# Feed-forward's second product: two of eight row pairs by seven block products in place of eight

## The chip, the cores and the metric

The kernel runs on one core of a Trainium2 chip. The metric is the device time of one execution in microseconds. Engines are named as in the profile: PE is the matrix engine (TensorE), PEld its weight loads, DVE is VectorE, ACT is ScalarE, SP is SyncE, whose queue issues the DMA transfers of the weights.

## The reference

One layer of an encoder over 256 tokens with a width of 2048. Only its last part matters here:

```python
def squared_relu_mlp(h, w1, w2):
    return jnp.square(jax.nn.relu(h @ w1)) @ w2
...
        x = x + squared_relu_mlp(rms_norm(x, norm_ffn_g[l]), w_ff1[l], w_ff2[l])
    return rms_norm(x, final_norm_g)
```

`w_ff1` is 2048 x 8192 and `w_ff2` is 8192 x 2048, both float32. Ahead of it come a gated convolution branch, an attention branch and a cross-attention, which the change leaves alone.

## The kernel before

Float32 products are made of three products in the format fp32r. Each operand is split into a high part (a rounded copy) and a low part (what is left); a product is high x high + high x low + low x high, all summed in PSUM.

**Units and the ring.** All weights pass through a ring of four slots (`RING = 4`) as units of 512 KB: two rows of 128 of the weight matrix, 512 columns wide, hence 1024 elements in each of 128 partitions. For each unit, in order:

1. SP loads it into `raw` (`load`, L372). Slot `u % 4` of `raw` is free when the low part of unit u - 4 is made (semaphore `lo_ready`).
2. ACT makes the high part `whi` (`hi`, L561). It waits for the load and for PE to be done with unit u - 4 (semaphore `used`).
3. DVE makes the low part `wlo` (`lo`, L931).
4. PE multiplies (`unit`, L1418 to L1420): 2 rows x 2 token halves x 3 products, 12 matmuls of 512 columns.

Every engine has one program order, written out by hand. ACT and DVE are three units ahead of PE (`LEAD = 3`): at step k of a stretch they split unit k + 3.

**Feed-forward.** The 8192 hidden columns are taken in four groups of 2048 (`GROUPS`). In each group the first product (`still_unit`, L1827 and L1829) takes 4 chunks of 8 units. Between it and the second product stand a few wide operations for each chunk: ACT's `ff_take` (L859), DVE's `ff_add` (L1324) and `ff_relus` (L1331), ACT's `ff_squares` and `ff_high`, DVE's `ff_low_part` (L1336). They leave the split hidden values in `c_hi` and `c_lo`, 16 tiles of 128 hidden columns x 256 tokens. The second product takes 4 chunks of 512 output columns, each 8 units, each chunk in two PSUM banks of its own, one for each half of the tokens. After each chunk DVE adds its two banks to the residual `xres` (L1375). In the last group the very last chunk is ordered so that the first token half ends earlier (`last_chunk`), and the final normalization follows it.

Of the kernel before, what the change touches and what calls it, by code (L numbers as in the profile page):

```python
# [7 lines left out]
ALU = mybir.AluOpType  # L8
# [120 lines left out]


def pair_of(n):

    return (n + 1) % 2
# [38 lines left out]
def build(nc, x, mem, positions, norm_mix_g, w_in, b_gate, conv_w, conv_b, conv_ln_g, conv_ln_b,  # L172
# [9 lines left out]
    with ExitStack() as ctx:  # L182
# [36 lines left out]
        fin_g = at(o + 8192, "fin_g", [P, D])  # L219
        fin = at(o + KS, "fin", [P, TT, D])  # L220

        o = cursor[0]
# [24 lines left out]
        rs_row = at(o, "rs_row", [P, SEQ])  # L247
        rs_diag = at(o + 1024, "rs_diag", [P, TT, P])

        o = cursor[0]  # L250
# [42 lines left out]
        def sem(name):  # L293
            return ctx.enter_context(nc.semaphore(name))
# [44 lines left out]
        rs_spread, rs_turned, rs_row_ready = (sem(n) for n in ("rs_spread", "rs_turned", "rs_row_ready"))  # L339
        ff_low, ff_sum, ff_relu, ff_square, ff_hi, ff_lo = (sem(n) for n in ("ff_low", "ff_sum", "ff_relu", "ff_square", "ff_hi", "ff_lo"))  # L340
        fin_landed, fin_gained = sem("fin_landed"), sem("fin_gained")
        tail_used, tail_added, tail_squared, tail_summed = (sem(n) for n in ("tail_used", "tail_added", "tail_squared", "tail_summed"))
# [25 lines left out]
        def _(sp):  # L368
            def load(u, r, src, kts=2, width=NC):

                wait(sp, lo_ready, u - RING + 1 + r)
                sp.dma_start(raw[:, u % RING, 0:kts * width].rearrange("p (k n) -> p k n", k=kts),  # L372
                             src).then_inc(landed[u % RING], 16)
# [55 lines left out]
            for n, (c, u) in enumerate(XO_ORDER):  # L429
                load(U_XO + n, 0, w_xo[:, 2 * u:2 * u + 2, NC * c:NC * (c + 1)])  # L430
            with sp.Fori(0, GROUPS) as g:
                r = g * FF_UNITS
                for c in range(CH):
                    load_chunk(U_FF + UPC * c, r, w_ff1, g * D + NC * c)
                for c in range(CH):
                    for k in range(UPC):
                        load(U_FF + UPC * (CH + c) + k, r, w_ff2[:, ds(g * KT + 2 * k, 2), NC * c:NC * (c + 1)])

# [116 lines left out]
        def _(act):  # L555
            def hi(u, r=0):

                s = u % RING
                act.wait_ge(landed[s], 16 * (u // RING + 1) + r * (16 // RING))
                wait(act, used, u - RING + 1 + r)  # L560
                act.activation(whi[:, s, :], raw[:, s, :], ACT.Copy).then_inc(hi_ready, 1)  # L561

            def turn_out(turn, dst, k0, gain=None, banks=(0, 1), first=6):
# [303 lines left out]
            def ff_high(c, done):  # L867
                act.wait_ge(ff_square, done)
                act.activation(c_hi[:, CPB * c:CPB * (c + 1), :], ff_row[:, c % 2, :, :], ACT.Copy).then_inc(ff_hi, 1)

            def ff_group(g, r, last, first=False):
                for c in range(CH):
                    for k in range(UPC):
                        hi(U_FF + UPC * c + k + LEAD, r)
                        if first and c == 0 and k == 1:
                            turn_out(T_X2 + CH - 1, a_hi, 4 * (CH - 1), V_FFN)
                        if first and c == 0 and k == 2:
                            x2_squares(CH - 1)
                        if first and c == 0 and k == 4:
                            act.wait_ge(sum_ready, 3)  # L880
                            root(sd_n, ss_sum, D)
                        if first and c == 0 and k == 7:
                            act.wait_ge(rs_turned, 1)
                            act.activation(rs_row[:], ps[:, 4, 0:SEQ], ACT.Copy, scale=float(D)).then_inc(rs_row_ready, 1)
                        if c and k == 1:
                            ff_squares(c - 1, g * CH + c)
                        if c and k == 2:
                            ff_high(c - 1, g * CH + c)
                    act.wait_ge(used, r + (U_FF + UPC * (c + 1)))
                    if c >= 2:  # L890
                        act.wait_ge(ff_lo, g * CH + (c - 1))
                    ff_take(c)
                for c in range(CH):
                    for k in range(UPC):
                        if not last or UPC * (CH + c) + k + LEAD < FF_UNITS:
                            hi(U_FF + UPC * (CH + c) + k + LEAD, r)
                        if c == 0 and k == 1:
                            ff_squares(CH - 1, g * CH + CH)
                        if c == 0 and k == 2:
                            ff_high(CH - 1, g * CH + CH)  # L900
                    if last and c < CH - 1:
                        act.wait_ge(chunk_out, N_FF + g * CH + c + 1)
                        chunk_squares(sq_res, xres[:, :, NC * c:NC * (c + 1)], c, SS_2 + TT * c)

# [21 lines left out]
        def _(dve):  # L926
            def lo(u, r=0):

                s = u % RING
                dve.wait_ge(hi_ready, u + 1 + r)  # L930
                dve.tensor_tensor(wlo[:, s, :], raw[:, s, :], whi[:, s, :].bitcast(F32), ALU.subtract).then_inc(lo_ready, 1)  # L931

            def bank_blocks(b):
# [399 lines left out]
            def ff_low_part(c, done):  # L1333
                dve.wait_ge(ff_hi, done)
                k = slice(CPB * c, CPB * (c + 1))
                dve.tensor_tensor(c_lo[:, k, :], ff_row[:, c % 2, :, :], c_hi[:, k, :].bitcast(F32), ALU.subtract).then_inc(ff_lo, 1)  # L1336

            def ff_group(g, r, last, first=False):
                for c in range(CH):
                    for k in range(UPC):  # L1340
                        if c and k == 0:
                            ff_add(c - 1, g * CH + c)
                        lo(U_FF + UPC * c + k + LEAD, r)
                        if first and c == 0 and k == 1:
# [12 lines left out]
                        if c and k == 2:  # L1357
                            ff_low_part(c - 1, g * CH + c)
                for c in range(CH):
                    for k in range(UPC):  # L1360
                        if c == 0 and k == 0:
                            ff_add(CH - 1, g * CH + CH)
                        if not last or UPC * (CH + c) + k + LEAD < FF_UNITS:
                            lo(U_FF + UPC * (CH + c) + k + LEAD, r)
                        if c == 0 and k == 0:
                            ff_relus(CH - 1, g * CH + CH)
                        if c == 0 and k == 2:
                            ff_low_part(CH - 1, g * CH + CH)
                        if last and k == 4 and c:

                            gain(c - 1)
                    if not last or c < CH - 1:
                        dve.wait_ge(used, r + (U_FF + UPC * (CH + c + 1)))
                        cols = xres[:, :, NC * c:NC * (c + 1)]
                        dve.tensor_tensor(cols, ps[:, 2 * c:2 * c + 2, :], cols, ALU.add).then_inc(chunk_out, 1)  # L1375

# [31 lines left out]
        def _(pe):  # L1408
# [392 lines left out]

            def last_chunk():
                p = 2 * (CH - 1)
                for k in range(UPC // 2):
                    unit(U_END - UPC + k, 0, c_hi, c_lo, 2 * k, p, k == 0, False)
                for t in range(TT):
                    tok = slice(P * t, P * (t + 1))
                    for k in range(UPC, KT):
# [5 lines left out]
                        mm = pe.matmul(ps[:, p + t, :], c_lo[:, k, tok], w_hi, start=False, stop=(k == KT - 1))  # L1814
                    mm.then_inc(tail_used, 1)

            def still_unit(u, r, k0, first, last, c):
# [14 lines left out]
            def ff_group(g, r, first=False, last=False):  # L1832
                for c in range(CH):
                    if c == 0:
                        pe.wait_ge(chunk_out, N_XO + 3 if first else g * CH + (N_FF - CH + 2))
                    elif c == 1:
                        pe.wait_ge(chunk_out, N_XO + CH if first else g * CH + N_FF)
                        if first:
                            pe.wait_ge(rs_row_ready, 1)
                    else:  # L1840
                        pe.wait_ge(ff_sum, g * CH + (c - 1))
                    for k in range(UPC):
# [6 lines left out]
                        if first and c == 0 and k == 6:  # L1849
# [3 lines left out]
                            mm.then_inc(rs_turned, 1)  # L1853
                for c in range(CH - last):
                    if c != 1:
                        pe.wait_ge(ff_sum, g * CH + (CH - 1 if c == 0 else CH))
                    for k in range(UPC):
                        if c == 0 and k % 2 == 0:
                            pe.wait_ge(ff_lo, g * CH + (k // 2 + 1))
                        unit(U_FF + UPC * (CH + c) + k, r, c_hi, c_lo, 2 * k, 2 * c, k == 0, k == UPC - 1)  # L1860

# [3 lines left out]
            ff_group(GROUPS - 1, (GROUPS - 1) * FF_UNITS, last=True)  # L1865
            last_chunk()

# [27 lines left out]
```

## Time and profile before

| | |
|---|---|
| median of 3 runs | 1624.31 us (1624.09 to 1624.81) |
| the profiled execution | 1623.88 us, its span 1622.1 us |
| PE busy | 1612.4 us (99% of the span) |
| DVE busy | 1102.8 us (68%) |
| ACT busy | 817.7 us (50%) |
| DMA | 304.97 MB, mean 188 GB/s |
| granted PE clock over the span | 0.999 |

The span is what the profile shows, from the first instruction to the last; the execution's own time is 1.8 us longer. Busy shares say how much of the span an engine had work. Which engine sets the time is read from the waits: an engine with no waits of its own is the bound.

### The profile page before, as it was taken

The page shows a single profiled execution, that of the slowest core. Times are in us where ns is not written, and L with a number is a line of the kernel's source. Part 1 is how long each engine was busy: PE and PEld are TensorE (multiplying, and loading weights), DVE is VectorE, ACT ScalarE, POOL GpSimd, SP SyncE. Part 2 cuts the span into 40 slices and gives each one's busy share as a digit, 9 for nine tenths or more (in the row PEclk, how much of TensorE's full clock was granted, in tenths as well). Part 3 has the DMA queues.
Part 4 walks back from the last instruction along what each step waited for, and adds up shares of the span by engine and source line. Part 5 has one row for each costly group of instructions (what it writes and reads, how often), then busy time and mean ns, then how long its engine had stood idle before and what let it go on. Part 6 is the DMA issues. An engine that isn't in the chain of part 4 may idle for free.

```text
span 1622.1 us, 22880 instructions
## 1 busy us (share of the span) xinstructions
PE 1612.4 (99%) x8210; PEld 1373.9 (85%) x8210; DVE 1102.8 (68%) x1494; ACT 817.7 (50%) x1046; POOL 70.6 (4%) x156
## 2 busy tenths in 40 slices
PE   9999999999999999999999999999999999999998
PEld 7888888888888888888889888888888888888886
DVE  5688889888888898665556656555555555546655
ACT  6444456555555556744446655334443454335543
POOL 6500010000000000000000000000000000000000
PEclk9999999999999999999999999999999999999999
DMA  7666655555555666667664566666666666666664
GB/s 250 203 190 186 189 160 170 174 176 179 177 163 175 216 201 192 185 191 254 188 193 146 167 185 193 194 195 182 195 194 192 187 188 194 193 191 192 185 189 145
DMA packets 161292, 304.97 MB, mean 188 GB/s; under 512 B 11689, under 2 KB 20513, under 8 KB 160801
## 3 DMA queue, kind: packets, MB, share of 16 engines
q1 hardware_dynamic: 160128, 300.45, 61.1%
q0 software_dynamic: 1056, 3.46, 0.6%
q8 instruction: 52, 0.85, 0.2%
q14 instruction: 24, 0.20, 0.0%
q10 hardware_dynamic: 32, 0.01, 0.0%
HBM read 301.78 MB, written 2.10 MB: 187 GB/s over the span
## 4 chain that ended last, share of the span: by engine, by line
PE 99%; ACT 0%; DVE 0%; DMA 0%; issue 0%; ACTq 0%
PE ps L1418 21%; PE ps L1420 21%; PE ps L1419 21%; PE ps L1827 15%; PE ps L1829 7%; PE ps L1431 1%; PE ps L1577 1%; PE ps L1576 1%; PE ps L1575 1%; PE ps L1630 1%; PE ps L1629 1%; PE ps L1600 0%; PE ps L1599 0%; PE ps L1598 0%; PE ps L1593 0%; PE ps L1592 0%
## 5 line engine op out<-in xcount | busy, mean ns | idle before, releaser
L931 DVE TENSOR_TENSOR wlo<-raw,whi 128x1024 fp32r<-128x1024 f32 x560 | 684.1, 1224 | 413.1 <-ACT whi L561 411.9
L561 ACT ACTIVATE whi<-raw 128x1024 fp32r<-128x1024 f32 x560 | 591.4, 1060 | 590.2 <-PE ps L1420 417.9
L1827 PE MATMUL ps<-a_both,whi 128*128 128x512 f32 x1024 | 321.7, 395 | 0.0
L1418 PE MATMUL ps<-whi,c_hi 128*128 128x512 f32 x752 | 293.3, 390 | 0.0
L1420 PE MATMUL ps<-whi,c_lo 128*128 128x512 f32 x752 | 292.6, 389 | 0.0
L1419 PE MATMUL ps<-wlo,c_hi 128*128 128x512 f32 x752 | 292.6, 389 | 0.0
L1418 PE MATMUL ps<-whi,a_both 128*128 128x512 f32 x700 | 277.1, 396 | 0.0
L1419 PE MATMUL ps<-wlo,a_both 128*128 128x512 f32 x700 | 272.7, 390 | 0.0
L1420 PE MATMUL ps<-whi,a_both 128*128 128x512 f32 x700 | 272.7, 390 | 0.0
L1829 PEld LDWEIGHTS ps<-a_both,wlo 128*128 128x128 f32 x1024 | 192.4, 188 | 45.4
L986 DVE SCALAR_TENSOR_TENSOR acc<-hconv,cwk,acc 128x256 f32<-128x256 f32 x464 | 205.0, 496 | 13.2 <-PE ps L1630 13.2
L1829 PE MATMUL ps<-a_both,wlo 128*128 128x256 f32 x1024 | 201.2, 278 | 0.0
L1420 PEld LDWEIGHTS ps<-whi,c_lo 128*128 128x128 f32 x752 | 141.2, 188 | 29.5
L1419 PEld LDWEIGHTS ps<-wlo,c_hi 128*128 128x128 f32 x752 | 141.2, 188 | 29.0
L1418 PEld LDWEIGHTS ps<-whi,c_hi 128*128 128x128 f32 x752 | 141.2, 188 | 28.5
L1827 PEld LDWEIGHTS ps<-a_both,whi 128*128 128x128 f32 x1024 | 156.2, 189 | 0.3
L1420 PEld LDWEIGHTS ps<-whi,a_both 128*128 128x128 f32 x700 | 131.4, 188 | 27.7
L1419 PEld LDWEIGHTS ps<-wlo,a_both 128*128 128x128 f32 x700 | 131.6, 188 | 25.8
L1418 PEld LDWEIGHTS ps<-whi,a_both 128*128 128x128 f32 x700 | 131.6, 188 | 25.8
L1324 DVE TENSOR_TENSOR ff_row<-ps,ff_row 128x1024 f32<-128x1024 f32 x16 | 19.6, 1225 | 24.4 <-ACT ff_row L859 24.4
L859 ACT ACTIVATE ff_row<-ps 128x1024 f32<-128x1024 f32 x16 | 16.4, 1026 | 27.3 <-PE ps L1829 27.3
L722 ACT ACTIVATE probs<-probs,stat 128x128 f32<-128x128 f32 (+1 forms) x32 | 17.2, 538 | 25.1 <-DVE stat L1104 25.1
(275 smaller groups left out, 1342.6 us busy)
## 6 DMA issues: line engine op xcount, KB each, us to landing
raw<-in_w_ff_dram SPq DMA_DIRECT2D x256, 512.0 KB, 4.0
raw<-in_w_in_dram SPq DMA_DIRECT2D x144, 512.0 KB, 3.7
raw<-in_w_mla_out_dram SPq DMA_DIRECT2D x32, 512.0 KB, 4.4
raw<-in_w_conv_out_dram SPq DMA_DIRECT2D x32, 512.0 KB, 4.3
raw<-in_w_out_dram SPq DMA_DIRECT2D x32, 512.0 KB, 4.3
raw<-in_w_ukv_dram SPq DMA_DIRECT2D x16, 512.0 KB, 3.8
raw<-in_w_xkv_dram SPq DMA_DIRECT2D x16, 512.0 KB, 3.9
raw<-in_w_uq_dram SPq DMA_DIRECT2D x16, 384.0 KB, 3.5
```

What stands on the lines that cost most here:

```text
L561: act.activation(whi[:, s, :], raw[:, s, :], ACT.Copy).then_inc(hi_ready, 1)
L722: act.activation(probs[:, h, a:b], probs[:, h, a:b], ACT.Exp, bias=ntop[:, n:n + 1], scale=qs[:, n % TT:n % TT + 1], accum_out=den[:, n:n ...
L859: act.activation(ff_row[:, c % 2, :, :], ps[:, ff1_banks(c), SEQ:], ACT.Copy).then_inc(ff_low, 1)
L931: dve.tensor_tensor(wlo[:, s, :], raw[:, s, :], whi[:, s, :].bitcast(F32), ALU.subtract).then_inc(lo_ready, 1)
L986: ins = dve.scalar_tensor_tensor(out=to, in0=h[:, tap:tap + SEQ], scalar=cwk[:, tap:tap + 1], in1=to, op0=ALU.mult, op1=ALU.add)
L1324: dve.tensor_tensor(row, ps[:, ff1_banks(c), 0:SEQ], row, ALU.add).then_inc(ff_sum, 1)
L1418: pe.matmul(sum_, x_hi[:, k0 + k, tok], w_hi, start=(first and k == 0), stop=False)
L1419: pe.matmul(sum_, x_hi[:, k0 + k, tok], w_lo, start=False, stop=False)
L1420: mm = pe.matmul(sum_, x_lo[:, k0 + k, tok], w_hi, start=False, stop=(last and k == kts - 1))
L1431: tr = pe.transpose(ps[:, first + b, SEQ * (k % 2) + P * t:SEQ * (k % 2) + P * (t + 1)], src[:, t, c0 + P * k:c0 + P * (k + 1)], ident[:])
L1827: pe.matmul(both, whi[:, s, cols[n]], a_both[:, :, k0 + k, :], start=(first and k == 0), stop=False)
L1829: mm = pe.matmul(ps[:, b0 + b + n, 0:SEQ], wlo[:, s, cols[n]], a_hi[:, k0 + k, :], start=False, stop=(last and k == 1))
```

## The change

The 16 units of two neighbouring chunks (a "pair", p = 0 or 1 in each group) are taken together, in an order of their own, `FF2_ORDER`; an entry (c, k) is chunk c of the pair and row k and k + 1 of the group's 16. For rows 0 to 3 (two row pairs, m = 0 and 1) the two token halves, the two rows of a pair and the two chunks make 2 x 2 blocks, and their product is made by seven block products in place of eight (Strassen's scheme in the form with 15 additions). The other twelve units are multiplied as before. The second pair of the last group (`plain`) keeps eight products. So seven pairs of eight are changed.

In each changed pair, positions 4 and 8 of the order (`LEFT`) hold the left chunk's units of rows 0, 1 and 2, 3, and positions 5 and 9 (`RIGHT`) the right chunk's. At a LEFT unit PE makes two block products (6 matmuls), at a RIGHT unit one (3 matmuls), and only the second half of a RIGHT unit is split. The other products need sums of weights, made by DVE from the raw units (`w_sums`, then the parts by ACT's `ws_high` and DVE's `ws_low`), and sums of hidden tiles (`h_sums`, made once for a group during the first product). They follow unit 11 (12 matmuls), unit 12 (6) and unit 13 (6). One partial sum goes into both chunks; ACT copies it out of its bank at two moments (`y_out`), and PE waits for these copies before it adds more. DVE adds to the residual in five steps in place of two. Loads 8, 9, 12 and 13 wait longer, since `w_sums` reads the raw slots.

```diff
+FF2_ORDER = ((0, 4), (0, 6), (1, 4), (1, 6), (0, 0), (1, 0), (0, 8), (0, 10),
+             (0, 2), (1, 2), (0, 12), (0, 14), (1, 8), (1, 10), (1, 12), (1, 14))
+LEFT, RIGHT = (4, 8), (5, 9)
+ONES_BANK, LAST_BANK = 4, 5
+FF2_BANKS = ((2, 0), (2, 6))
...
+                for p in range(2):
+                    for i, (c, k) in enumerate(FF2_ORDER):
+                        n = 2 * p + c
+                        after = {8: 6, 9: 6, 12: 11, 13: 11}.get(i, i - RING)
+                        load(U_FF + UPC * CH + FF2_UNITS * p + i, r, w_ff2[:, ds(g * KT + k, 2), NC * n:NC * (n + 1)], later=after - (i - RING))
...
+            def ws_high(g, p, m):
+                act.wait_ge(ws_made, g * 12 + (6 * p + 3 * (m + 1)))
+                for half in (1, 0):
+                    act.activation(ws_hi[m][half][:], w_sum[:, 2 * NC * half:2 * NC * (half + 1)], ACT.Copy).then_inc(ws_hi_ready, 1)
+            def y_out(g, p, n):
+                if n == 0 and p:
+                    act.wait_ge(mixed, g * 6 + 1)
+                act.wait_ge(y_step, g * 6 + (3 * p + n + 1))
+                act.activation(y_copy[:, n, :], ps[:, ONES_BANK, :], ACT.Copy).then_inc(y_copied, 1)
...
+                    for k in range(FF2_UNITS):
+                        n = UPC * CH + FF2_UNITS * p + k + LEAD
+                        if k + LEAD in RIGHT and not plain:
+                            hi_second(U_FF + n, r)
+                        elif not last or n < FF_UNITS:
+                            hi(U_FF + n, r)
...
+                        if k in (3, 8) and not plain:
+                            ws_high(g, p, k // 8)
+                        if k in (9, 12) and not plain:
+                            y_out(g, p, (9, 12).index(k))
...
+            def w_sums(g, p, m, s):
...
+                wait(dve, ws_lo_ready, g * 8 + (4 * p + 2 * m))
+                dve.tensor_tensor(t1_t3.rearrange("p (b n) -> p b n", b=2), right.rearrange("p (b n) -> p b n", b=2), raw[:, s:s + 2, 0:NC],
+                                  ALU.subtract).then_inc(ws_made, 1)
+                dve.wait_ge(ws_made, g * 12 + (done + 1))
+                dve.tensor_tensor(t2, right[:, NC:], t1, ALU.subtract).then_inc(ws_made, 1)
+                dve.wait_ge(ws_made, g * 12 + (done + 2))
+                dve.tensor_tensor(t4, left[:, NC:], t2, ALU.subtract).then_inc(ws_made, 1)
...
+                        if i in RIGHT and not plain:
+                            lo_second(U_FF + u + i, r)
+                        elif not last or u + i < FF_UNITS:
+                            lo(U_FF + u + i, r)
...
+                            if k in (2, 7):
+                                w_sums(g, p, k // 7, (U_FF + u + LEFT[k // 7]) % RING)
+                            if k in (3, 4):
+                                ws_low(g, p, 0, 4 - k)
+                            if k in (8, 9):
+                                ws_low(g, p, 1, 9 - k)
+                            if k == 12:
+                                add_copies(g, p)
+                            if k == 13:
+                                add_ones(g, p)
+                                dve.wait_ge(p4_done, g * 2 + (p + 1))
+                                dve.wait_ge(mixed, g * 6 + (3 * p + 1))
+                                add_chunk(p, 0)
+                            if k == 14:
+                                add_last(g, p)
...
+                    if i == 11:
+                        pe.wait_ge(ws_lo_ready, g * 8 + (4 * p + 3))
+                        pe.wait_ge(y_copied, g * 4 + (2 * p + 1))
+                        for m in range(2):
+                            mm = product(ONES_BANK, *combined(1, m), *weight_sum(2, m), last=(m == 1))
+                        mm.then_inc(y_step, 1)
+                        for m in range(2):
+                            mm = product(banks[0] + 1, *hidden(2 * m + 1, 1), *weight_sum(3, m), last=(m == 1))
+                        mm.then_inc(p4_done, 1)
+                    if i == 12:
+                        pe.wait_ge(ws_lo_ready, g * 8 + (4 * p + 4))
+                        pe.wait_ge(y_copied, g * 4 + (2 * p + 2))
+                        for m in range(2):
+                            mm = product(ONES_BANK, *combined(0, m), *weight_sum(0, m), last=(m == 1))
+                        mm.then_inc(y_step, 1)
+                    if i == 13:
+                        for m in range(2):
+                            mm = product(LAST_BANK, *combined(2, m), *weight_sum(1, m), first=(m == 0), last=(m == 1))
+                        mm.then_inc(p7_done, 1)
```

`product` is three matmuls of 512 columns. In ACT's and DVE's programs, what stands under `if k == ...` comes behind the split of unit k + 3 in the same step.

## Rows read from the trace of the kernel before

**Rows 1.** The page: busy time of the engines, and the chain that ended last.

```profile
PE 1612.4 (99%) x8210; PEld 1373.9 (85%) x8210; DVE 1102.8 (68%) x1494; ACT 817.7 (50%) x1046; POOL 70.6 (4%) x156
...
PE 99%; ACT 0%; DVE 0%; DMA 0%; issue 0%; ACTq 0%
```

**Rows 2.** Who waited for whom, PE alone, whole span, longest first.

```profile
PE ps L1446 <- POOL stat L460: 1.5, 1, 1.5
```

**Rows 3.** Busy time in one chunk of the second product (us, count; clock, DMA).

```profile
1041.26:1063.02 21.76, 21.76 (x98) 18.02 (x97) 10.96 (x9) 8.48 (x9) 0.00 (x0) 1.00 0.64 194
```

**Rows 4.** Timeline around one unit of the second product: start us, us, engine.

```profile
1074.11 1.23 DVE L931 TENSOR_TENSOR wlo<-raw,whi 128x1024 fp32r<-128x1024 f32 x1 [1.50 <-ACT whi L561]
...
1075.47 0.39 PE L1418 MATMUL ps<-whi,c_hi 128*128 128x512 f32 x1
...
1075.49 8.53 SPq L372 DMA_DIRECT2D raw<-in_w_ff_dram  x4
...
1075.73 1.06 ACT L561 ACTIVATE whi<-raw 128x1024 fp32r<-128x1024 f32 x1 [1.66 <-PE ps L1420]
...
1076.83 1.23 DVE L931 TENSOR_TENSOR wlo<-raw,whi 128x1024 fp32r<-128x1024 f32 x1 [1.50 <-ACT whi L561]
...
1078.19 0.39 PE L1418 MATMUL ps<-whi,c_hi 128*128 128x512 f32 x1
```

**Rows 5.** Groups of instructions by line, feed-forward stretch: busy us, mean ns.

```profile
L931 DVE TENSOR_TENSOR wlo<-raw,whi 128x1024 fp32r<-128x1024 f32 x256 | 313.1, 1224 | 279.0 <-ACT whi L561 279.0
L561 ACT ACTIVATE whi<-raw 128x1024 fp32r<-128x1024 f32 x256 | 271.1, 1060 | 325.6 <-PE ps L1420 180.4 <-PE ps L1829 145.1
...
L1336 DVE TENSOR_TENSOR c_lo<-ff_row,c_hi 128x1024 fp32r<-128x1024 f32 x16 | 19.5, 1219 | 0.0
L1375 DVE TENSOR_TENSOR xres<-ps,xres 128x1024 f32<-128x1024 f32 x15 | 18.4, 1225 | 5.6 <-PE ps L1420 5.6
...
L859 ACT ACTIVATE ff_row<-ps 128x1024 f32<-128x1024 f32 x16 | 16.4, 1026 | 27.3 <-PE ps L1829 27.3
L592 ACT ACTIVATE sq_res<-xres 128x512 f32<-128x512 f32 x12 | 7.5, 634 | 8.6 <-DVE xres L1375 8.6
...
L1316 DVE TENSOR_TENSOR fin<-xres,fin_g 128x512 f32<-128x512 f32 x6 | 3.9, 684 | 0.0
```

**Rows 6.** DMA issues on the page, and the summary of the tile `raw`.

```profile
raw<-in_w_ff_dram SPq DMA_DIRECT2D x256, 512.0 KB, 4.0
...
DMA to landing us min/median/max: 3.3/3.9/9.3
```

**Rows 7.** DMA issues near 742 us: KB each, us to landing.

```profile
xres<-in_x_dram SPq DMA_DIRECT2D x1, 2048.0 KB, 9.0
raw<-in_w_conv_out_dram SPq DMA_DIRECT2D x1, 512.0 KB, 4.3
...
raw<-in_w_out_dram SPq DMA_DIRECT2D x1, 512.0 KB, 9.3
```

**Rows 8.** SP's queue in order of time near 742 us.

```profile
742.56 0.47 SPq L423 DMA_DIRECT2D xres<-in_x_dram  x1
743.63 90.73 SPq L372 DMA_DIRECT2D raw<-in_w_out_dram  x32
```

**Rows 9.** Busy time and granted clock (after the engines) at the end.

```profile
1617.00:1618.00 1.00, 0.00 (x0) 0.00 (x0) 0.96 (x4) 0.88 (x2) 0.00 (x0) 0.86 0.00 0
1618.00:1619.00 1.00, 0.00 (x0) 0.00 (x0) 0.13 (x1) 0.45 (x1) 0.00 (x0) 0.50 0.57 197
```

**Rows 10.** Timeline: the last matmul.

```profile
1614.77 0.39 PE L1814 MATMUL ps<-whi,c_lo 128*128 128x512 f32 x1
```

**Rows 11.** Timeline of PE at the start of the program.

```profile
6.36 0.77 PE L1455 MATMUL ps<-whi,a_both 128*128 128x512 f32 x1 [0.70 <-ACT whi L618]
...
7.88 0.78 PE L1455 MATMUL ps<-wlo,a_both 128*128 128x512 f32 x1
...
10.56 0.39 PE L1455 MATMUL ps<-whi,a_both 128*128 128x512 f32 x1
```

More of the change, by code:

```diff
@@ L1358, in ff_group @@
                             ff_low_part(c - 1, g * CH + c)
-                for c in range(CH):
-                    for k in range(UPC):
-                        if c == 0 and k == 0:
-                            ff_add(CH - 1, g * CH + CH)
-                        if not last or UPC * (CH + c) + k + LEAD < FF_UNITS:
-                            lo(U_FF + UPC * (CH + c) + k + LEAD, r)
-                        if c == 0 and k == 0:
+                for p in range(2):
+                    plain = last and p == 1
+                    u = UPC * CH + FF2_UNITS * p
+                    for k in range(FF2_UNITS):
+                        if p == 0 and k == 0:
+                            ff_add(CH - 1, g * CH + CH)
+                        i = k + LEAD
+                        if i in RIGHT and not plain:
+                            lo_second(U_FF + u + i, r)
+                        elif not last or u + i < FF_UNITS:
+                            lo(U_FF + u + i, r)
+                        if p == 0 and k == 0:
@@ L1377, in _ @@
+                    if not plain:
+                        dve.wait_ge(used, r + (U_FF + u + FF2_UNITS))
+                        dve.wait_ge(mixed, g * 6 + (3 * p + 3))
+                        add_chunk(p, 1)
             ff_group(0, 0, False, True)
@@ L1798, in _, with last_pair @@
                     turn(T_X2 + c, xres, NC * c, split_out(T_X2 + c - 1) if c else None)
[L1802 to L1805, printed above, removed]
+            def last_pair():
+                u = U_END - FF2_UNITS
+                for i, (c, k) in enumerate(FF2_ORDER[:FF2_UNITS - 4]):
+                    unit(u + i, 0, c_hi, c_lo, k, FF2_BANKS[1][c], i in (0, 2), i == 11)
+                p = FF2_BANKS[1][1]
                 for t in range(TT):
@@ L1815, in last_chunk, with product, seven_pair, hidden @@
                     mm.then_inc(tail_used, 1)
+            def product(bank, x_hi, x_lo, w_hi, w_lo, first=False, last=False):
+                pe.matmul(ps[:, bank, :], x_hi, w_hi, start=first, stop=False, skip_group_check=True)
+                pe.matmul(ps[:, bank, :], x_hi, w_lo, start=False, stop=False, skip_group_check=True)
+                return pe.matmul(ps[:, bank, :], x_lo, w_hi, start=False, stop=last, skip_group_check=True)
+            def seven_pair(g, r, p):
+                u = U_FF + UPC * CH + FF2_UNITS * p
+                banks = FF2_BANKS[p]
+                def hidden(k, t):
+                    tok = slice(P * t, P * (t + 1))
+                    return c_hi[:, k, tok], c_lo[:, k, tok]
+                def combined(n, m):
+                    return h_hi[:, n, m, :], h_lo[:, n, m, :]
+                def slot(i, half):
+                    cols = slice(NC * half, NC * (half + 1))
+                    return whi[:, (u + i) % RING, cols], wlo[:, (u + i) % RING, cols]
+                def weight_sum(n, m):
+                    cols = slice(NC * (n % 2), NC * (n % 2 + 1))
+                    return ws_hi[m][n // 2][:, cols], ws_lo[m][n // 2][:, cols]
+                for i, (c, k) in enumerate(FF2_ORDER):
+                    pe.wait_ge(lo_ready, u + i + 1 + r)
+                    if p == 0:
+                        pe.wait_ge(ff_lo, g * CH + (k // 4 + 1))
+                    if i in LEFT:
+                        m = LEFT.index(i)
+                        if i == LEFT[0] and p == 0:
+                            pe.wait_ge(ff_sum, g * CH + CH)
+                        if i == LEFT[0] and p:
+                            pe.wait_ge(mixed, g * 6 + 3)
+                        mm = product(ONES_BANK, *hidden(2 * m, 0), *slot(i, 0), first=(m == 0), last=(m == 1))
+                        if m == 1:
+                            mm.then_inc(y_step, 1)
+                        product(banks[0], *hidden(2 * m + 1, 0), *slot(i, 1)).then_inc(used, 1)
+                    elif i in RIGHT:
+                        m = RIGHT.index(i)
+                        pe.wait_ge(h_lo_ready, g + 1)
+                        product(banks[1], *combined(3, m), *slot(i, 1)).then_inc(used, 1)
+                    else:
+                        for n in range(2):
+                            for t in range(TT):
+                                ends = n == 1 and (i == 15 or (i == 11 and t == 0))
+                                mm = product(banks[c] + t, *hidden(k + n, t), *slot(i, n), first=(i in (0, 2) and n == 0), last=ends)
+                        mm.then_inc(used, 1)
+                    if i == 11:
[12 more added lines that the diff above has]
+                            mm = product(ONES_BANK, *combined(0, m), *weight_sum(0, m), last=(m == 1))
+                        mm.then_inc(y_step, 1)
+                    if i == 13:
+                        for m in range(2):
+                            mm = product(LAST_BANK, *combined(2, m), *weight_sum(1, m), first=(m == 0), last=(m == 1))
+                        mm.then_inc(p7_done, 1)
@@ L1853, in ff_group @@
                             mm.then_inc(rs_turned, 1)
[L1854 to L1860, printed above, removed]
+                pe.wait_ge(ff_sum, g * CH + (CH - 1))
+                seven_pair(g, r, 0)
+                pe.wait_ge(chunk_out, g * CH + (N_FF + 1))
+                if last:
+                    last_pair()
+                else:
+                    seven_pair(g, r, 1)
             ff_group(0, 0, True)
```

121 lines of the change are left out of this document (96 added, 25 removed).

## The prediction

> **What bounds the kernel now.** I read the page first: PE is busy in 99% of the span and the chain that ended last lies on PE [rows 1]. Busy time alone does not prove a bound, so next the waits of PE: the longest in the whole span is 1.5 us, before the first weights are there [rows 2]. So a matmul less is time saved, as long as nobody comes late. In one chunk of the second product (21.76 us, 96 matmuls, so 0.2267 us each) DVE works 10.96 us, ACT 8.48, and the transfers take 0.64 of the DMA engines' time [rows 3]. There seems to be room. Whether the room is at the right places the averages don't say; that needs the order of the work.
>
> The timeline shows the rhythm. A unit is 2.72 us of PE (1075.47 to 1078.19). ACT starts on the slot set free 0.26 us after the next unit's first matmul, DVE 0.04 us after ACT's end, SP's next load 0.15 us after DVE's end (1074.11 + 1.23 = 1075.34, load at 1075.49) [rows 4]. So unit u + 4 is split 2.6 us after PE leaves unit u, and PE comes to it 8.2 us after leaving u (three units): cover of 5.6 us. That reserve is what the change spends.
>
> **What it saves.** A changed pair has 12 units of 12 matmuls and 14 block products of 3: 186 for 192. Seven pairs: 42 matmuls x 0.2267 = 9.5 us. The Trainium skill ("TensorE: Matmul & The Clock Gate", Back-to-back issue gap) has 216 ns for 512 columns; by it this would be 9.1 us. The trace decides for 0.2267.
>
> **What it adds to DVE and ACT.** Durations: DVE 1.22 us for 1024 elements, 0.68 for 512; ACT 1.06 and 0.63 [rows 5]. Hence in a changed pair DVE has 14 x 1.22 + 2 x 0.68 of splits, 2 x (1.22 + 2 x 0.68 + 2 x 1.22) of sums and their low parts, 5 x 1.22 of adding out: 34.6 us, and 38.3 in a group's first pair with `ff_add`, `ff_relus` and `ff_low_part`; before, 22 for the pair. PE's pair without waits is 186 x 0.2267 = 42.16 (before 43.52). ACT comes to about 21.6. Neither engine is full, so I cost this work by its place alone. `h_sums` and their split (about 4 x 0.42 + 1.22 on DVE, 1.06 on ACT, an estimate for the 256-element ones) lie in the first product, where nothing is compressed: nothing, covered by that 5.6 us reserve; without cover under 4 us a group.
>
> **Where it waits.** Second pair of a group, time 0 at its first matmul. Without waits PE would come to unit 4 at 10.88, 6 at 12.92, 8 at 18.36, 10 at 20.40, 11 at 23.12: units 4, 5, 8 and 9 are 6, 3, 6 and 3 matmuls long, so six units pass in 9.5 us in place of 16.3, and the reserve is gone by unit 10.
>
> DVE has the half split of unit 5 done at 7.05, then `w_sums` (1.22 + 0.68 + 0.68 and hops of 0.04) to 9.74, low part 6 to 11.01. Load 8 had to wait for that (in the old order it would have waited for low part 4, at 5.3), and 9 and 10 stand behind it. How long a load takes: 3.3 us at least, the feed-forward's median 4.0 [rows 6], 4.3 with more traffic behind it; I take 4.1. Those behind land in order 1.37 us apart: the 2 MB transfer issued at 742.56 landed after 9.0 (751.56), the 512 KB one behind it, issued at 743.63, after 9.3 (752.93) [rows 7, 8]. So 8, 9, 10 land at 15.3, 16.6, 18.0, load 11 (after low part 7, 14.3) at 19.4. Low part 8 is there at 17.6 (needed 18.36), 10 at 20.38 (needed 20.40). Now `w_sums` again stands ahead of low part 11: 20.42 to 23.09, and low part 11 ends at 24.36. PE waits 1.26 us at unit 11.
>
> Then the main step. After unit 11 PE wants `y_copied`. ACT makes that copy at step 9 behind `hi` of unit 12, and load 12 waits for low part 11. The chain is 24.36, load issued 24.51, landed 28.61, high part 29.71, copy 30.38, PE goes on at 30.40. Unit 11 ended at 27.12: a wait of 3.28 us. Behind it stand unit 12's matmuls and everything else on PE. From here 72 matmuls remain, 16.32 us; their operands are early (low part 12 at 30.9, 13 at 33, the second copy at 34.5 for 36). The pair ends at 46.72: 3.20 us more than before.
>
> In a group's first pair `ff_add` and `ff_relus` push low part 6 to 11.52; the same chain then gives low part 11 at 24.87, PE on at 30.91, end at 47.23: +3.71. The `plain` pair also has the late loads 8 and 12, but no short units: low part 12 at about 30.7 for unit 12 at 32.64, so nothing; cover gone only if a load took 2 us more.
>
> Sum: 4 x 3.71 + 3 x 3.20 = +24.4 us (waits of 34 less the 9.5 saved).
>
> **The clock.** PE's array stands still some 3.1 us in each such wait. At the end of the kernel the granted clock fell (0.86 in the slice from 1617, 0.50 after, so from 2.4 to 1.2 GHz at 1617.7) [rows 9], 2.6 us after the last matmul had ended at 1615.16 [rows 10]. A fall here costs matmuls at half speed afterwards. At the start, where matmuls of 512 columns took 0.77 us, they did so from 6.36 until after 7.88 and 0.39 from 10.56 (the clock column doesn't show this) [rows 11]: some 3.7 us of work at the lower level, 1.9 lost. Nothing in between shows how a wait of 3 us inside dense work is treated, so the bounds are none of seven falls (0) and all (13.3 us). I take three, fewer than half, because the wait is only half a us longer than the one fall seen: +5.7. The Trainium skill says in the same page (HAM oscillation) that idle gaps bring the array back to half rate and cost half of the time spent there; by it the direction is the same, and rows 9 agree with the fall.
>
> **Sum.** 24.4 + 5.7 = 30.1 us onto the profiled execution's 1623.88 (its span 1622.1 and 1.8 around it): 1654.0. The median of the runs is 0.43 above that execution, so 1654.4.
>
> **Rivals.**
> 1. Waits as above, clock never or once lower: 1624.3 + 24.4 = 1648.7. For it: waits of 3 us lie between dense stretches. Against: rows 9, 10.
> 2. The clock falls in nearly every wait: 24.4 + 13.3, 1662.
> 3. Shorter fetches: at 3.3 us a load, both waits shrink and the pairs cost 1.6 and 2.1 more: +13.2, 1637.5. Against: three or four loads issued together, not one alone.
> 4. The wait for `y_copied` doesn't bind, since ACT gets to its copy in time. Then the pair loses 3.28 us: -0.08 and +0.43, together +1.5, 1625.8, no change. It would need the time from low part 11 to the copy, 6.0 us in my sum, to be 2.8; the load alone has never taken under 3.3.
> 5. Other side, one mechanism: the ring's reserve lasts, so low part 11 is there before 23.1 and the copy before unit 11 is over. Then only the 42 matmuls count: 1624.3 - 9.5 = 1614.8. It decides where PE goes on after unit 11 before 27.2 (43.52 less 16.32); I have 30.4. For it only the low averages of rows 3.
>
> **Chances.** Forecast case (waits, two to four falls) 0.35; rival 1 0.28; rival 2 0.17; rival 3 0.12; rival 4 0.04; rival 5 0.04. A difference of 0.2% (3.2 us) is about what a measurement of this kernel can tell from none; rival 4 is inside it, rival 5 beyond it on the fast side, all others slower. So faster 0.04, same 0.04, slower 0.92. A load of 4.8 us in place of 4.1 adds 1.4 a pair, 10 in all. The range 1637 to 1664 holds the first four cases but for their edges, at most 0.2 outside. The size hangs on fetch time and clock, the sign on neither.
>
> **What would show it.** In the profile after: PE with two waits in each of seven pairs, about 1.3 us (DVE's low part, unit 11) and 3.3 us (ACT's copy, before the 12 matmuls behind unit 11), nothing in the last pair; pairs 46.7 to 47.2 us long; 42 matmuls fewer; ACT waiting for the load of unit 12; granted clock under 0.999, by 0.5 x 3.7 us for each fall. If PE shows no waits of over 2 us in the changed pairs, the argument is wrong at the order of ACT's copy; if the waits are right and the time isn't, at the clock.

## The result and the profile after

The change makes the kernel slower: 1657.57 us (median of 4 runs, 1654.94 to 1657.80) against 1624.53 us, a ratio of 1.0202 with a 95% interval of 1.0189 to 1.0214. The profiled execution took 1657.75 us, its span 1655.9; before, the span was 1622.1.

The page of the changed kernel, busy time and the chain that ended last, beside [rows 1]:

```profile
PE 1620.6 (98%) x8168; PEld 1373.0 (83%) x8168; DVE 1192.8 (72%) x1605; ACT 849.3 (51%) x1092; POOL 70.8 (4%) x156
...
PE 87%; DMA 4%; DVE 4%; issue 2%; ACT 2%; SPq 0%; ACTq 0%; DVEq 0%
```

PE is still 98% busy, with 42 matmuls fewer (8168 for 8210), and nothing in the busy line says that the kernel lost 33 us. The chain says it: 13% of it now lies off PE.

Who waited for whom, PE alone (us in total, times, longest), beside [rows 2]:

```profile
PE ps L1976 <- ACT y_copy L914: 20.7, 7, 3.2
PE ps L1976 <- DVE wlo L993: 4.9, 7, 0.7
```

Seven waits for the copy and seven for a low part, one of each in every changed pair. The columns give the idle time of an engine whose matmuls overlap; from one matmul's start to the next, the gap before the copy is used is 3.2 to 3.6 us where 0.23 is normal.

The chain in order of time, second pair of the first group (start us, us, what):

```profile
1052.95 1.15 DVE w_sum L1422
...
1055.54 1.15 DVE wlo L993
...
1057.95 6.00 DMA raw<-in_w_ff_dram
1063.98 1.07 ACT whi L586
1065.07 1.23 DVE wlo L993
1066.30 1.15 DVE w_sum L1422
...
1067.47 0.70 DVE w_sum L1425
...
1068.19 0.69 DVE w_sum L1427
1068.89 1.14 DVE wlo L993
...
1070.18 4.20 DMA raw<-in_w_ff_dram
...
1075.37 0.59 ACT y_copy L914
...
1076.09 0.76 PE ps L1976
```

This is the prediction's chain, read from below. PE goes on at 1076.09, after the copy (1075.37), after the high part of unit 12, after its fetch (4.20 us from 1070.18), after low part 11 (1068.89), which stood behind the weight sums (1066.30 to 1068.89), behind low part 10, whose fetch had itself been held by the first sums. From the start of low part 11 to PE's next matmul 7.2 us pass, of which one unit of PE (2.72) is cover. That ACT stood at the fetch, and not PE or DVE at ACT, is this line of ACT's timeline; the copy comes right behind it:

```profile
1074.41 1.06 ACT L586 ACTIVATE whi<-raw 128x1024 fp32r<-128x1024 f32 x1 [3.48 <-DMA raw<-in_w_ff_dram]
```

The timeline of PE at that point:

```profile
1072.47 0.39 PE L1977 MATMUL ps<-wlo,c_hi 128*128 128x512 f32 x1
1072.70 0.39 PE L1978 MATMUL ps<-whi,c_lo 128*128 128x512 f32 x1
1076.09 0.76 PE L1976 MATMUL ps<-ws,h_hi 128*128 128x512 f32 x1 [3.01 <-ACT y_copy L914]
1076.66 0.63 PE L1977 MATMUL ps<-ws,h_hi 128*128 128x512 f32 x1
1077.08 0.63 PE L1978 MATMUL ps<-ws,h_lo 128*128 128x512 f32 x1
```

After the gap from 1072.70 to 1076.09 the matmuls stand 0.42 to 0.43 us apart and no longer 0.23. That is the lower clock. The granted clock (after the busy times of the five engines) in 3 us just behind each of the seven waits:

```profile
1029.50:1032.50 3.00, 3.00 (x13) 2.50 (x14) 3.00 (x4) 2.42 (x3) 0.00 (x0) 1.00 0.84 276
1076.10:1079.10 3.00, 3.00 (x7) 2.42 (x8) 3.00 (x4) 2.58 (x3) 0.00 (x0) 0.50 0.87 278
1215.10:1218.10 3.00, 3.00 (x8) 2.37 (x9) 3.00 (x4) 2.54 (x3) 0.00 (x0) 0.55 0.75 250
1263.40:1266.40 3.00, 3.00 (x7) 2.40 (x8) 3.00 (x4) 2.58 (x3) 0.00 (x0) 0.50 0.83 249
1400.40:1403.40 3.00, 3.00 (x7) 2.42 (x8) 3.00 (x4) 2.58 (x3) 0.00 (x0) 0.50 0.84 263
1451.00:1454.00 3.00, 3.00 (x9) 2.33 (x8) 3.00 (x4) 2.55 (x3) 0.00 (x0) 0.50 0.79 227
1587.50:1590.50 3.00, 3.00 (x8) 2.32 (x8) 3.00 (x4) 2.08 (x3) 0.00 (x0) 0.50 0.90 291
```

It fell at six waits of seven, to 0.50; 1.00 and 0.50 are 2.4 and 1.2 GHz. Three of the falls came while PE still waited, three up to 1 us after it had gone on (the row from 1451.00 starts 1 us behind the wait's end, where the fall was), all of them 2.2 to 3.9 us after the last matmul before the wait had ended. The length of the gap does not tell which wait brings a fall: the shortest, 3.16 us, did and one of 3.22 us did not. The number also differs between executions of this kernel: the fastest of the four, 1654.94 us, has a mean granted clock of 0.993 where the others have 0.991, which by an estimate is one or two falls less.

Adding up, over the seven pairs: what PE's gaps exceed the normal 0.2267 us comes to 31.1 us, matmuls at the lower clock beyond 0.2267 us each to 11.4 us, and 42 matmuls fewer give 9.5 back: 33.0 of the 33.8 us by which the span grew. The remaining 0.8 us is not accounted for.

### The profile page after: what moved, and what is told of

Its sections match the earlier page's. It is cut to its first block, busy times and chain, and to the rows that moved or that the text cites. A ratio compares the mean times of both kernels' runs of the same rounds, so it can differ in the third digit from the quotient of the medians.

```text
span 1655.9 us, 23075 instructions
## 1 busy us (share of the span) xinstructions
PE 1620.6 (98%) x8168; PEld 1373.0 (83%) x8168; DVE 1192.8 (72%) x1605; ACT 849.3 (51%) x1092; POOL 70.8 (4%) x156
## 4 chain that ended last, share of the span: by engine, by line
PE 87%; DMA 4%; DVE 4%; issue 2%; ACT 2%; SPq 0%; ACTq 0%; DVEq 0%
PE ps L1575 15%; PE ps L1577 15%; PE ps L1576 15%; PE ps L2054 14%; PE ps L2056 7%; DMA raw<-in_w_ff_dram 4%; PE ps L1976 3%; PE ps L1977 3%; PE ps L1978 3%; DVE wlo L993 1%; PE ps L1588 1%; DVE w_sum L1422 1%; PE ps L1734 1%; PE ps L1733 1%; PE ps L1732 1%
## 5 line engine op out<-in xcount | busy, mean ns | idle before, releaser
L993 DVE TENSOR_TENSOR wlo<-raw,whi 128x1024 fp32r<-128x1024 f32 x546 | 665.9, 1225 | 354.6 <-ACT whi L586 353.0
L586 ACT ACTIVATE whi<-raw 128x1024 fp32r<-128x1024 f32 x546 | 576.5, 1060 | 571.5 <-PE ps L1577 245.0
L1976 PE MATMUL ps<-whi,c_hi 128*128 128x512 f32 x364 | 143.6, 394 | 5.0 <-DVE wlo L993 4.9
L1977 PE MATMUL ps<-wlo,c_hi 128*128 128x512 f32 x364 | 142.3, 391 | 0.0
L1978 PE MATMUL ps<-whi,c_lo 128*128 128x512 f32 x364 | 141.8, 390 | 0.0
L1575 PE MATMUL ps<-whi,c_hi 128*128 128x512 f32 x304 | 119.0, 391 | 0.0
L1577 PE MATMUL ps<-whi,c_lo 128*128 128x512 f32 x304 | 118.4, 389 | 0.0
L1576 PE MATMUL ps<-wlo,c_hi 128*128 128x512 f32 x304 | 118.3, 389 | 0.0
L1976 PEld LDWEIGHTS ps<-whi,c_hi 128*128 128x128 f32 x364 | 68.8, 189 | 24.1 <-DVE wlo L993 9.9
L1978 PEld LDWEIGHTS ps<-whi,c_lo 128*128 128x128 f32 x364 | 68.6, 188 | 14.6
L1977 PEld LDWEIGHTS ps<-wlo,c_hi 128*128 128x128 f32 x364 | 68.6, 189 | 13.8
```

What stands on the lines that cost most here:

```text
L1575: pe.matmul(sum_, x_hi[:, k0 + k, tok], w_hi, start=(first and k == 0), stop=False)
L1576: pe.matmul(sum_, x_hi[:, k0 + k, tok], w_lo, start=False, stop=False)
L1577: mm = pe.matmul(sum_, x_lo[:, k0 + k, tok], w_hi, start=False, stop=(last and k == kts - 1))
L1976: pe.matmul(ps[:, bank, :], x_hi, w_hi, start=first, stop=False, skip_group_check=True)
L1977: pe.matmul(ps[:, bank, :], x_hi, w_lo, start=False, stop=False, skip_group_check=True)
L1978: return pe.matmul(ps[:, bank, :], x_lo, w_hi, start=False, stop=last, skip_group_check=True)
```

## The experiments

In all of them the kernel before was measured on the same chip; its medians were 1624.4 us in the first four and 1624.17 us in the last four.

### 1. Fill the wait with matmuls: what does the clock cost?

```diff
                         pe.wait_ge(ws_lo_ready, g * 8 + (4 * p + 3))
+                        if p:
+                            pe.wait_ge(chunk_out, g * CH + (N_FF + 2))
+                        spare = ps[:, (6, 0)[p], :].rearrange("p (k s) -> p k s", k=2)
+                        for _ in range(12):
+                            pe.matmul(spare, c_hi[:, 0, 0:P], c_hi[:, 0:2, :], start=True, stop=True, skip_group_check=True)
                         pe.wait_ge(y_copied, g * 4 + (2 * p + 1))
```

> The changed kernel with 12 more matmuls of 512 columns (2.72 us, into a PSUM bank that is free, their results unused) just before PE waits for the copy behind unit 11. They take PE's time only where it waits anyway. Theory (the long wait lets the granted clock fall, and this costs about 11 us beside the waits): no fall of the clock in the feed-forward, the wait for the copy down to about 0.5 us, 1657.6 - 11 = 1646 us. Rival (the lower clock is a mere record, or the price of the change lies in the waits alone): 1655 to 1658 us, no gain.

Measured: 1645.95 us (1645.10 to 1647.27), ratio to before 1.0136 (1.0119 to 1.0153). The waits of PE:

```profile
PE ps L1976 <- DVE wlo L993: 4.7, 7, 0.7
...
PE ps L1976 <- ACT y_copy L914: 0.8, 4, 0.2
```

84 matmuls more, and 11.6 us less. Every fall in the feed-forward is gone (mean granted clock 0.999, in the changed kernel 0.991). The copy is as late as before; the work in the gap only keeps PE busy. So the lower clock was real time, a third of the loss, and the remaining 21.5 us are the waits less the 9.5 saved.

### 2. The copy ahead of unit 12's high part

```diff
+                        if k == 9 and not plain:
+                            y_out(g, p, 0)
                         if k + LEAD in RIGHT and not plain:
                             hi_second(U_FF + n, r)
...
-                        if k in (9, 12) and not plain:
-                            y_out(g, p, (9, 12).index(k))
+                        if k == 10 and not plain:
+                            y_out(g, p, 1)
```

> The changed kernel with ACT's first copy put ahead of the high part of unit 12 and its second behind that of unit 13; nothing else moved. Theory (the copy stands behind a fetch that could not be made in time): the wait of 3 us before the 12 matmuls behind unit 11 is gone, PE still waits 1.0 to 1.7 us at unit 11 and now about 1.15 us for the low part of unit 12, whose load is as late as before; no falls of the clock; 1634 us. Rival (DVE simply has too much work, so the wait goes elsewhere in full): 1650 us or more.

Measured: 1631.70 us (1630.40 to 1633.28), ratio 1.0043 (1.0026 to 1.0059). The waits of PE:

```profile
PE ps L1978 <- DVE wlo L995: 11.7, 14, 1.1
```

Two copies moved in ACT's program give 25.9 us back. Part of that is the clock, which no longer falls in the feed-forward; experiment 1 put its price at 11.6 us. No wait for the copy is left; there are 14 waits for a low part, up to 1.1 us: at unit 11 as before, and at unit 12, whose fetch is as late as ever but is now covered in part by the 12 matmuls ahead of it. So about 1 us a pair of the old wait moves to unit 12, not all of it, and the rival (DVE's total load, by which it would move in full) falls: DVE's work is the same.

### 3. The weight sums earlier in DVE's program

```diff
-                        after = {8: 6, 9: 6, 12: 11, 13: 11}.get(i, i - RING)
+                        after = {12: 10, 13: 10}.get(i, i - RING)
...
+                for i in (LEFT[m], RIGHT[m]):
+                    n = U_FF + UPC * CH + FF2_UNITS * p + i
+                    dve.wait_ge(landed[n % RING], 16 * (n // RING + 1) + r * (16 // RING))
...
+                        if k in (1, 7) and not plain:
+                            w_sums(g, p, k // 7, (U_FF + u + LEFT[k // 7]) % RING, r)
                         if i in RIGHT and not plain:
                             lo_second(U_FF + u + i, r)
...
-                            if k in (2, 7):
-                                w_sums(g, p, k // 7, (U_FF + u + LEFT[k // 7]) % RING)
```

> The changed kernel with the same work, but DVE makes the first weight sums before the low part of unit 4 and the second before the low part of unit 10 (it waits for the loads itself), so that loads 8 and 9 go out as early as in the old order and loads 12 and 13 behind low part 10. Theory (the ring's reserve is lost by the place of the sums, not by their amount): no waits of PE in the changed pairs over 0.3 us, 1624.3 - 9.5 = 1615 us. Rival A (DVE's load or the shorter units as such take the reserve): over 1630. Rival B (the fetch rate, three loads within 5 us): waits move to unit 10, 1620 to 1630.

Measured: 1620.27 us (1619.79 to 1621.32), ratio 0.9975 (0.9965 to 0.9985): 4.1 us faster than before, a small difference but one that its interval keeps from none, and 37.3 us faster than the change. The waits of PE:

```profile
PE ps L1979 <- ACT y_copy L914: 0.9, 4, 0.3
PE ps L1979 <- DVE wlo L993: 0.8, 4, 0.2
```

The same work in another order. The sums read raw units that had landed some 3 us before; made one or two steps earlier, they hold back neither the loads nor the low parts that PE wants next. The 5 us that are missing to the expected 1615 are small waits: four of 0.24 us or less at unit 10 of the groups' first pairs, and one of up to 0.3 us for the copy in every pair; counted from start to start with the restart, together 4.7 us. Each restart costs beyond the wait itself: the first matmul after one stands 0.31 to 0.34 us ahead of the next in this trace, not 0.23.

### 4. The order and the late loads, without the scheme

All pairs take `unit` for all 16 units; no sums, copies or additional adding out.

```diff
+            def plain_pair(g, r, p):
+                u = U_FF + UPC * CH + FF2_UNITS * p
+                for i, (c, k) in enumerate(FF2_ORDER):
...
+                    unit(u + i, r, c_hi, c_lo, k, FF2_BANKS[p][c], i in (0, 2), i in (11, 15))
...
-                seven_pair(g, r, 0)
+                plain_pair(g, r, 0)
```

> The new order of the units, the late loads 8, 9, 12 and 13 and the new banks, but all pairs with eight block products: no sums, no copies, 192 matmuls a pair. Theory: the late loads alone cost nothing, since without short units PE comes to unit 12 about 2 us after its low part is there: 1624 us, as before. Rival (the order or the late loads cost something by themselves): each pair longer by up to 1 us, 1627 to 1632.

Measured: 1624.64 us (1624.12 to 1625.62), ratio 1.0002 (0.9992 to 1.0011). PE had no wait in the feed-forward. Order, banks and late loads are free as long as every unit is 12 matmuls long.

### 5. Sums early and copy early

Experiment 3, and in ACT's program `y_out(g, p, 0)` ahead of `hi` at step 9 (the second copy stays at step 12).

> The kernel with the sums early (it measured 1620.3), and in addition ACT makes the first copy ahead of the high part of unit 12. Theory: the seven small waits before the 12 matmuls behind unit 11 (0.3 to 0.45 us each beyond the matmuls' own spacing) are gone, the four in the groups' first pairs at unit 10 (0.5 us each with the restart, low part 10 behind the second sums) stay: 1620.3 - 2.7 = 1617.6 us. Rival (the copy's place no longer matters, what is left is the restart of DVE's chain): 1620 us as before.

Measured: 1618.36 us (1617.44 to 1618.68), ratio 0.9962 (0.9948 to 0.9975). PE's waits in the pairs:

```profile
PE ps L1981 <- DVE wlo L995: 0.8, 4, 0.2
```

These are the four at unit 10 of the groups' first pairs. The timeline of DVE ahead of the first of them shows why they stay (part of a stretch from 1000.77 to 1021.4 in which it pauses once, for 0.47 us):

```profile
1011.33 1.22 DVE L1437 TENSOR_TENSOR ws<-w_sum,ws 128x1024 fp32r<-128x1024 f32 x1
1012.46 1.22 DVE L995 TENSOR_TENSOR wlo<-raw,whi 128x1024 fp32r<-128x1024 f32 x1
1013.60 1.22 DVE L1437 TENSOR_TENSOR ws_a<-w_sum,ws_a 128x1024 fp32r<-128x1024 f32 x1
1014.73 1.22 DVE L995 TENSOR_TENSOR wlo<-raw,whi 128x1024 fp32r<-128x1024 f32 x1
1015.87 0.68 DVE L1001 TENSOR_TENSOR wlo<-raw,whi 128x512 fp32r<-128x512 f32 x1
1016.47 1.22 DVE L1427 TENSOR_TENSOR w_sum<-raw 128x1024 f32<-128x1024 f32 x1
...
1019.06 2.35 DVE L995 TENSOR_TENSOR wlo<-raw,whi 128x1024 fp32r<-128x1024 f32 x2
```

DVE works without a gap until low part 10 (the first of the two from 1019.06). This is the best version found, 5.8 us faster than before where the matmuls left out are worth 9.5. Once the sums are in place, the copy's place is worth only 1.9 us more.

### 6. More work for DVE at the same places

Experiment 5, and ahead of each set of sums twice a subtraction of 512 elements into a tile that nobody reads:

```diff
+                spare = cw[:].rearrange("p a b -> p (a b)")
+                for n in range(2):
+                    wait(dve, extra, g * 8 + (4 * p + 2 * m + n))
+                    dve.tensor_tensor(spare, right[:, NC:], left[:, NC:], ALU.subtract).then_inc(extra, 1)
```

> As the kernel with sums and copy early, plus two more DVE subtractions of 512 elements ahead of each set of weight sums, into a tile that nobody reads: 2 x 0.72 us more in each of 14 places. It tests amount against place. Theory (DVE has no cover left at unit 10 of a group's first pair, some 0.5 us to 1 us at that of the second): waits at unit 10 of 1.9 us in four pairs and 0.5 to 1 us in three, 1617.6 + 7 = 1625 us. Rival (place is all that counts, the amount is hidden): under 1619 us.

Measured: 1631.65 us (1630.70 to 1632.71), ratio 1.0047 (1.0031 to 1.0062). The waits of PE:

```profile
PE ps L1986 <- DVE wlo L996: 12.3, 7, 2.4
```

1.4 us more for each set, 20 us in all, and 13.3 of them reach the end. The expectation was right in kind and 6.6 us short: the gaps are 2.7 us in a first pair and 1.3 to 1.4 in a second. The timeline of DVE shows why. In a first pair it now works from 1001.75 to 1024.4 with no pause at all, so what was added to both sets (1.33 us each) reaches low part 10, less the one pause of 0.47 us that experiment 5 had: 2.2 us, and the gaps grew by 2.1 to 2.2. In a second pair the addition to the first set goes into a pause ahead of low part 6 (2.45 us in experiment 5, 1.28 here), and only that to the second set arrives: the gap is 1.1 to 1.2 us beyond the spacing. So the amount counts as well once the places are right: in a second pair some 0.2 us of reserve is left behind the second sums, in a first none.

### 7. The second sums alone earlier

Experiment 3 without moving the first sums (they stay behind low part 5, loads 8 and 9 behind low part 6).

> The changed kernel with the second weight sums alone ahead of low part 10, loads 12 and 13 behind low part 10; the first sums, loads 8 and 9 and ACT's copies stay as in the change. By the same timeline as the prediction: low part 10 at 22.3 for 20.40 (a wait of 1.9 us in a second pair, some 2.5 in a first), the copy at 28.2 for 27.8 (0.4 us): each pair 1.0 to 1.6 us longer than before, no fall of the clock, 1633 us. Rival (the second sums are the whole cause): 1620 us, as with both early.

Measured: 1629.68 us (1629.26 to 1630.05), ratio 1.0032 (1.0020 to 1.0044). The waits of PE:

```profile
PE ps L1981 <- DVE wlo L993: 9.1, 7, 1.9
PE ps L1981 <- ACT y_copy L914: 1.7, 6, 0.3
```

The waits come where they were expected, at unit 10 (gaps of 1.3 to 2.3 us) and before the copy (0.5 to 0.7 us), a little smaller, so that the time is 3.3 us under the 1633 expected. Both places count: moving the second sums gives 27.9 us, moving the first as well 9.4 more.

### 8. The weight sums on GpSimd

`w_sums` becomes part of GpSimd's program with the same three subtractions; SP waits for `ws_made` ahead of loads 8 and 12; the copy is early as in experiment 5.

```diff
+                pool.tensor_tensor(t1_t3.rearrange("p (b n) -> p b n", b=2), right.rearrange("p (b n) -> p b n", b=2), raw[:, s:s + 2, 0:NC],
+                                   ALU.subtract).then_inc(ws_made, 1)
...
+                        if i in (8, 12) and not (final and p):
+                            sp.wait_ge(ws_made, g * 12 + (6 * p + 3 * (i // 4 - 1)))
```

> All weight sums made by GpSimd, which is idle in this stretch, in place of DVE; the loads 8, 9 and 12, 13 wait for the sums by their own semaphore, the first copy ahead of the high part of unit 12. A GpSimd operation of 256 elements took 0.84 us and one of 64 0.59, so an estimate of 1.9 and 1.2 us for 1024 and 512 elements, 4.2 us for a set in place of 2.7. Theory (DVE's 5.3 us a pair are taken off, and nothing else is late): no waits of PE in the pairs, 1615 to 1616 us. Rival (GpSimd slower than that estimate, or slowing DVE's operations beside it): sums later than 17.7 us into the pair, loads 12 and 13 late again, over 1620 us.

Measured: 1633.32 us (1631.87 to 1637.26), ratio 1.0057 (1.0044 to 1.0071), so 15 us slower than with the sums on DVE. The waits of PE:

```profile
PE ps L2001 <- DVE wlo L1020: 6.5, 8, 1.3
PE ps L2001 <- ACT y_copy L939: 3.5, 3, 1.3
PE ps L2001 <- DVE wlo L1026: 2.5, 4, 0.7
```

GpSimd's groups by line (busy us, mean ns), then DVE's in the same stretch:

```profile
L590 POOL TENSOR_TENSOR w_sum<-raw 128x1024 f32<-128x1024 f32 x14 | 40.6, 2896 | 694.9 <-DMA raw<-in_w_ff_dram 638.4 <-DVE ws_a L1459 56.6
L595 POOL TENSOR_TENSOR w_sum<-raw,w_sum 128x512 f32<-128x512 f32 x14 | 30.1, 2152 | 1.1
L593 POOL TENSOR_TENSOR w_sum<-raw,w_sum 128x512 f32<-128x512 f32 x14 | 26.4, 1887 | 1.1
```

```profile
L1020 DVE TENSOR_TENSOR wlo<-raw,whi 128x1024 fp32r<-128x1024 f32 x209 | 280.6, 1350 | 158.8 <-ACT whi L611 158.5
L1026 DVE TENSOR_TENSOR wlo<-raw,whi 128x512 fp32r<-128x512 f32 x14 | 26.4, 1887 | 2.8 <-ACT whi L618 2.8
...
L1489 DVE TENSOR_TENSOR xres<-ps,xres 128x1024 f32<-128x1024 f32 x14 | 17.1, 1219 | 2.6 <-PE ps L2003 2.6
```

A set of sums takes GpSimd 6.9 us, not the 4.2 estimated, where DVE needs 2.6. And DVE pays too: its half splits take 1887 ns on average (0.69 us in experiment 5) and its whole splits 1350 for 1223. The growth is in those that run beside GpSimd: from 985 us on, 38 whole splits overlap with it and take 1.92 us on average, the other 174 take 1.22. The adding out that reads PSUM (L1489) does not grow: three of its instructions lie wholly inside one of GpSimd's and take 1.22 us like the rest. One meeting of each kind in the timeline:

```profile
1016.05 3.24 POOL L590 TENSOR_TENSOR w_sum<-raw 128x1024 f32<-128x1024 f32 x1 [6.40 <-DVE ws_a L1459]
...
1016.94 2.90 DVE L1026 TENSOR_TENSOR wlo<-raw,whi 128x512 fp32r<-128x512 f32 x1
...
1045.07 2.63 POOL L590 TENSOR_TENSOR w_sum<-raw 128x1024 f32<-128x1024 f32 x1 [21.86 <-DMA raw<-in_w_ff_dram]
1045.78 1.22 DVE L1489 TENSOR_TENSOR xres<-ps,xres 128x1024 f32<-128x1024 f32 x1 [0.34 <-PE ps L2003]
```

The Trainium skill ("SBUF — State Buffer", Who interferes with whom) says that a VectorE instruction with two SBUF inputs and a GpSimd instruction that reads SBUF lock each other out. By that rule it is the two-input splits that grow and not the one with an input in PSUM, and the trace agrees: beside GpSimd 1.92 us on average for a whole split against 1.22 for the adding out of as many elements.

The granted clock fell once in this run's feed-forward, at 1201.0, in the second of two gaps close together (1.09 and 1.64 us), so that a wait of 3 us is not needed for a fall.

## Why the prediction was right

**The result.** 1657.57 us against a forecast of 1654.4, inside the range of 1637 to 1664, on the side that had 0.92. That it came within 3.2 us is in part luck: the waits were forecast 3 us too long and the clock's share 5.7 us too short, and the two partly cancel. Of the cases listed, the mechanism was the forecast's; the number of falls was that of rival 2.

**What it saves** held: 42 matmuls fewer in the page, 9.5 us in the sum above.

**Where it waits** held in place and in chain. Unit 11 was forecast to wait 1.26 us; its gap is 1.05 to 1.11 us, which is 0.9 beyond the spacing. The wait for the copy was forecast at 3.28 us; the gaps are 3.2 to 3.6, 3.0 to 3.4 beyond the spacing. Low part 11 to PE's next matmul: 6.04 us forecast, 6.06 found (1070.03, where low part 11 ends, to 1076.09). All waits: 34 us forecast, 31.1 found. Two things make the excess. The 0.51 us that `ff_add` and `ff_relus` were to add in each group's first pair are not there: the gaps at unit 11 are 1.07 to 1.11 us in first pairs and 1.05 to 1.10 in second ones (2.0 us of the sum). And I charged 1.22 us for each of DVE's operations, while in the chain above one follows another after 1.14 or 1.15 us. What each restart costs beyond its wait, 0.1 us, was in no term; it is part of the 31.1. The fetch was nearly as forecast: from the end of low part 6 (1056.69) to the landing of load 10 (1063.95) 7.26 us, where the forecast had 18.0 less 11.01, 6.99.

**The clock** held in size for one fall (1.9 us forecast, 11.4 / 6 = 1.9 found) and not in number: six falls, not three. This term, 5.7 for 11.4, is the larger miss of the sum, and experiment 1 shows it alone: 11.6 us. I had taken "fewer than half" because the only fall seen came 2.6 us after the last matmul and the waits were only half a us longer. The falls came 2.2 to 3.9 us after the last matmul's end and some of them after PE had gone on, so comparing the wait's length with 2.6 us was no ground for a number; what decides whether a wait brings a fall stays open.

**Rivals.** The one with hardly any fall (1648.7) is out by the clock rows; the one with nearly all (1662) is what happened to the clock, and is 4.4 us too high, most of it in the waits. Shorter fetches: out, 4.2 us at the median for 4.0. The rival that the copy does not bind (1625.8) is what experiment 2 builds, at 1631.7: it takes more than the copy's place to come to no change, since unit 12 then waits. The rival with the reserve intact is out for this kernel, and experiments 3 and 5 show that it was a matter of order: 1620.3 and 1618.4, of the 1614.8 that the matmuls alone would give.

**The step at nothing.** The sums of hidden tiles in the first product and the `plain` pair cost nothing that the profile shows: PE waits in neither.

## What to carry to other kernels

A saving on the engine that bounds the kernel shortens its units, and with that the cover that every fetch and split behind it had; count the reserve in time of that engine at each position of the ring, not in busy shares. When a helper's result is wanted, list what stands ahead of it in its engine's program order: here a copy of 0.6 us stood behind a fetch it did not need, and moving it was worth 26 us, the clock included. Gains of such repairs do not add up: with the sums in place (37 us) moving the first copy gave 1.9 us. Where the matrix engine must wait some 3 us, its clock may well fall (six times of seven here); price that beside the wait.

## What the runs showed of the hardware

- Gaps of 3.2 to 3.6 us between matmuls inside dense work went with a fall of TensorE's granted clock from 1.00 to 0.50 in six cases of seven; 84 matmuls with unused results in those gaps bought 11.6 us. Four gaps of 2.7 us (experiment 6) brought no fall, and two of 1.1 and 1.6 us close together (experiment 8) brought one.
- At the full clock the first matmul after a wait stands 0.31 to 0.34 us ahead of the next one instead of 0.23, even where the wait was 0.2 us.
- VectorE's operations with two operands in SBUF grow beside GpSimd's subtractions from SBUF: a split of 512 elements took 0.69 us in experiment 5 and up to 2.90 beside GpSimd, while those with an operand in PSUM stayed at 1.22 us for 1024 elements. GpSimd needed 2.90 us for 1024 elements on average; how much of that it would need alone is not shown.
